# Thirty-two experts in pairs: a tensor engine program written out with constant waits, its block bounds read one pair ahead

## The reference, cut to what matters

```python
for e in range(N_EXPERTS):                      # 32
    hid = jax.nn.silu(t @ w_gate[e]) * (t @ w_up[e])     # 1024 -> 256
    out = out + combine[:, e:e + 1] * (hid @ w_down[e])  # 256 -> 1024
```

## Time and profile before

| | |
|---|---|
| runs | 565.57 us median of 3 (564.02 to 568.11) |
| the profiled execution's own time | 564.8 us |
| its span | 563.0 us (1.8 us lie around it) |
| PE busy | 489.6 us, 87% |
| DMA moved | 141.69 MB, 252 GB/s over the span |
| mean granted TensorE clock | 0.959 |

### The profile page before, as it was taken

One profiled execution on the slowest core, in us unless ns is written; L12 is line 12 of the kernel. 1 busy time (PEld: TensorE's weight loads), 2 busy tenths in 40 slices (PEclk: granted clock), 3 DMA queues, 4 the chain that ended last, 5 costly groups with the idle time before them and its releaser, 6 DMA issues.

```text
span 563.0 us, 9101 instructions
## 1 busy us (share of the span) xinstructions
PE 489.6 (87%) x3407; PEld 294.1 (52%) x3408; DVE 247.8 (44%) x478; ACT 108.5 (19%) x230; POOL 187.2 (33%) x282
## 2 busy tenths in 40 slices
PE   6999999999999999996489889898878687388972
PEld 4887777777776455453244444444434343244430
DVE  4139999999945223368222212222121212022236
ACT  5130111111125211121122112121111112012214
POOL 2014728836768001110423333332313313033100
PEclk9999999999999999996799999999989989699988
DMA  8993016000003991029678999999999999998076
GB/s 331 333 399 57 0 57 243 2 0 1 1 1 118 376 415 42 37 87 401 220 293 286 366 383 403 397 398 391 396 384 382 391 394 390 396 402 353 30 284 227
DMA packets 35504, 141.69 MB, mean 252 GB/s; under 512 B 10194, under 2 KB 10210, under 8 KB 23193
## 3 DMA queue, kind: packets, MB, share of 16 engines
q1 hardware_dynamic: 29194, 127.91, 59.8%
q0 software_dynamic: 4960, 9.45, 5.2%
q10 hardware_dynamic: 1327, 4.01, 1.8%
HBM read 134.99 MB, written 13.17 MB: 263 GB/s over the span
## 4 chain that ended last, share of the span: by engine, by line
PE 69%; DMA 15%; DVE 4%; SPq 4%; issue 4%; ACT 3%; ACTq 0%; POOL 0%; POOLq 0%; DVEq 0%
PE bank L1218 25%; PE bank L1301 9%; PE bank L1412 9%; PE bank L1432 8%; PE bank L1407 7%; DMA region_x<-in_w_up 6%; DMA region_w<-in_w_up 5%; SPq L383 4%; PE bank L1211 3%; DMA out<-sb_rows 2%; PE bank L1398 2%; PE bank L1362 1%; PE bank L1422 1%; PE bank L1327 1%; DVE ua L1109 1%
## 5 line engine op out<-in xcount | busy, mean ns | idle before, releaser
L1218 PE MATMUL bank<-region_h,region_w 128*128 128x256 f32 (+1 forms) x576 | 140.6, 406 | 0.0
L1218 PEld LDWEIGHTS bank<-region_h,region_w 128*128 128x128 f32 x576 | 109.2, 190 | 29.8
L1109 DVE TENSOR_TENSOR ua<-ua,bank 128x128 f32<-128x128 f32 x30 | 8.6, 286 | 191.0 <-ACT ua L616 191.0
L1412 PE MATMUL bank<-region_w,z 128*32 128x256 f32 x512 | 47.1, 419 | 14.6 <-DMA region_w<-in_w_up 12.3
L1301 PE MATMUL bank<-region_w,z 128*128 128x512 f32 x128 | 56.7, 596 | 0.2 <-ACT z L559 0.2
L1432 PE MATMUL bank<-region_w,ua 128*32 128x512 f32 x344 | 51.9, 598 | 0.0
L772 POOL COPY gcol<-gidx 64x1 uint32 (+1 forms) x30 | 5.3, 178 | 135.3 <-DVE sb_rows L1104 135.3
L894 DVE SCALAR_TENSOR_TENSOR z<-ub,par,z 128x512 f32<-128x512 f32 x60 | 47.5, 791 | 0.0
L894 DVE SCALAR_TENSOR_TENSOR region_x<-ub,par,region_x 128x512 f32<-128x512 f32 x56 | 46.5, 831 | 0.0
L703 POOL TENSOR_TENSOR ub<-region_x 128x512 f32<-128x512 f32 x4 | 25.3, 6320 | 57.8 <-ACT ub L513 31.1
L1301 PEld LDWEIGHTS bank<-region_w,z 128*128 128x128 f32 x128 | 23.8, 190 | 28.0 <-issue 26.3
(11 more groups left out here) (231 smaller groups left out, 628.3 us busy)
## 6 DMA issues: line engine op xcount, KB each, us to landing
region_w<-in_w_down SPq DMA_DIRECT2D x21, 1024.0 KB, 18.2
region_w<-in_w_gate SPq DMA_DIRECT2D x16, 1024.0 KB, 15.1
region_w<-in_w_up SPq DMA_DIRECT2D x16, 1024.0 KB, 17.1
region_w<-in_w_in SPq DMA_DIRECT2D x4, 2048.0 KB, 18.6
slot<-in_w_gate SPq DMA_DIRECT2D x6, 1024.0 KB, 14.8
slot<-in_w_up SPq DMA_DIRECT2D x6, 1024.0 KB, 14.4
slot<-in_w_down SPq DMA_DIRECT2D x6, 1024.0 KB, 14.8
region_x<-in_w_up SPq DMA_DIRECT2D x5, 1024.0 KB, 26.7
```

What stands on the lines that cost most here:

```text
L1218: ins = mm(ps[2 * bank + j][:, 0:LEN[j]], sec[name][:, k, c * P:(c + 1) * P], hT[:, k, CUT[j]], start=(k == 0), stop=(k == KC - 1))
L1412: ins = mm(ps[1][r0:r0 + H, 0:2 * P].rearrange("p (w f) -> p w f", w=2), xT[:, k, half * H:(half + 1) * H], wgu[i][:, :, k, h, :], start=( ...
```

## The change

- On TensorE the loop over slots goes. All 16 pairs are written out, and every wait on a weight has a constant (`turn_of(e) * 16 + 16`). The inner loops over own blocks stay, and so do their `If`s.
- The three reads of `bound` at the start of each pair go. The first pair's two bounds are read ahead of the wait for the first tokens (`mine = bounds(0)`); its first block is the constant 0, and later each pair's first block is the pair before's end, which is in a register. The bounds of pair m+1 are read in the shared block of pair m, behind the token transposes and ahead of the wait for the hidden rows.
- On SP the 26 reloads are written out, with constant slots, constant expert numbers in the DMAs' addresses and a constant place in `bound`. Each still reads one bound, waits as before and issues the same three DMAs in the same order.

```diff
             def load_part(i, part, e):
                 dst = ...
-                sp.dma_start(dst, parts[part][:, bass.ds(e, 1), :].rearrange("p e n -> p (e n)"))\
-                  .then_inc(s_wexp[i][part], 16)
+                sp.dma_start(dst, parts[part][:, e, :]).then_inc(s_wexp[i][part], 16)
...
-            with sp.Fori(1, NE // NSLOT) as it:
-                for i in range(NSLOT):
-                    reload(it, i)
-            for i in range(NE % NSLOT):
-                reload(NE // NSLOT, i)
+            for e in range(NSLOT, NE):
+                last = sp.value_load(bound[0:1, e - NSLOT + 1:e - NSLOT + 2], min_val=1, max_val=NBLK)
+                sp.wait_ge(s_gu, last)
+                load_part(slot_of(e), 0, e)
+                load_part(slot_of(e), 1, e)
+                sp.wait_ge(s_down, last)
+                load_part(slot_of(e), 2, e)
...
+            def bounds(m):
+                return [pe.value_load(bound[0:1, 2 * m + j:2 * m + j + 1], min_val=1, max_val=NBLK) for j in (1, 2)]
...
                 tr(ps[2][:, 0:P], hid, ident[:, :]).then_inc(s_hT_ps, 1)
                 tokens(KC // 2, KC).then_inc(s_xt_ps, 1)
+                ahead = meanwhile() if meanwhile else None
                 pe.wait_ge(s_hidT, g + 1)
...
             keep_busy(18)
             pe.wait_ge(s_tab, 1)
+            mine = bounds(0)
             pe.wait_ge(s_mv, 1)
             tokens(0, KC).then_inc(s_xt_ps, 1)
...
-            def pair(it, i):
-                e = it * NSLOT + i
-                first = pe.value_load(bound[0:1, bass.ds(e, 1)], min_val=0, max_val=NBLK - 1)
-                after = pe.value_load(bound[0:1, bass.ds(e + 1, 1)], min_val=1, max_val=NBLK)
-                end = pe.value_load(bound[0:1, bass.ds(e + 2, 1)], min_val=1, max_val=NBLK)
+            def pair(m, first, after, end):
+                e = 2 * m
...
-                block_of(after - 1, (i, i + 1), it)
+                ahead = block_of(after - 1, (e, e + 1), (lambda: bounds(m + 1)) if m + 1 < NPAIR else None)
...
-            with pe.Fori(0, NE // NSLOT) as it:
-                for i in range(0, NSLOT, 2):
-                    pair(it, i)
-            for i in range(0, NE % NSLOT, 2):
-                pair(NE // NSLOT, i)
+            first = 0
+            for m in range(NPAIR):
+                after, end = mine
+                mine = pair(m, first, after, end)
+                first = end
```

More of the change, by code:

```diff
@@ L87, in build_step, with slot_of, turn_of @@
                   (RX, D, ub_t, D)]
+        def slot_of(e):
+            return e % NSLOT
+        def turn_of(e):
+            return e // NSLOT
         slot_gu = [reg[:, lo:lo + 2 * PART] for reg, lo, _, _ in places]
@@ L1399, in tokens, with block_of @@
                 return ins
-            def block_of(g, halves, turn):
+            def bounds(m):
+                return [pe.value_load(bound[0:1, 2 * m + j:2 * m + j + 1], min_val=1, max_val=NBLK) for j in (1, 2)]
+            def block_of(g, experts, meanwhile=None):
+                halves = [slot_of(e) for e in experts]
                 pe.wait_ge(s_xt, g + 1)
@@ L1423, in block_of @@
                 tokens(KC // 2, KC).then_inc(s_xt_ps, 1)
+                ahead = meanwhile() if meanwhile else None
                 pe.wait_ge(s_hidT, g + 1)
                 pe.wait_ge(s_yc, g + 1)
-                for i in sorted(set(halves)):
-                    pe.wait_ge(s_wexp[i][2], turn * 16 + 16)
+                for e in sorted(set(experts)):
+                    pe.wait_ge(s_wexp[slot_of(e)][2], turn_of(e) * 16 + 16)
                 for c in range(F // P):
@@ L1435, in block_of @@
                 ins.then_inc(s_down, 1)
+                return ahead
             keep_busy(18)
             pe.wait_ge(s_tab, 1)
+            mine = bounds(0)
             pe.wait_ge(s_mv, 1)
             tokens(0, KC).then_inc(s_xt_ps, 1)
-            def pair(it, i):
-                e = it * NSLOT + i
-                first = pe.value_load(bound[0:1, bass.ds(e, 1)], min_val=0, max_val=NBLK - 1)
-                after = pe.value_load(bound[0:1, bass.ds(e + 1, 1)], min_val=1, max_val=NBLK)
-                end = pe.value_load(bound[0:1, bass.ds(e + 2, 1)], min_val=1, max_val=NBLK)
+            def pair(m, first, after, end):
+                e = 2 * m
                 for part in range(2):
-                    pe.wait_ge(s_wexp[i][part], it * 16 + 16)
+                    pe.wait_ge(s_wexp[slot_of(e)][part], turn_of(e) * 16 + 16)
                 with pe.If(after > first + 1):
                     with pe.Fori(first, after - 1) as g:
-                        block_of(g, (i, i), it)
+                        block_of(g, (e, e))
                 for part in range(2):
-                    pe.wait_ge(s_wexp[i + 1][part], it * 16 + 16)
-                block_of(after - 1, (i, i + 1), it)
+                    pe.wait_ge(s_wexp[slot_of(e + 1)][part], turn_of(e + 1) * 16 + 16)
+                ahead = block_of(after - 1, (e, e + 1), (lambda: bounds(m + 1)) if m + 1 < NPAIR else None)
                 with pe.If(end > after):
                     with pe.Fori(after, end) as g:
-                        block_of(g, (i + 1, i + 1), it)
-            with pe.Fori(0, NE // NSLOT) as it:
-                for i in range(0, NSLOT, 2):
-                    pair(it, i)
-            for i in range(0, NE % NSLOT, 2):
-                pair(NE // NSLOT, i)
+                        block_of(g, (e + 1, e + 1))
+                return ahead
+            first = 0
[3 more added lines that the diff above has]
+                first = end
             pe.wait_ge(s_diag, 2 * len(BY_PE))
```

## The result

The changed kernel takes 570.6 us (median of 14 runs, 568.13 to 574.64), the one before 567.92 us (14 runs on the same chips): ratio 1.0047, 95% interval 1.0024 to 1.0070. Measured again on another chip it was 573.48 against 566.51 us: 1.0128 (1.0106 to 1.0151). So it is slower, by 0.5% to 1.3%; the forecast was 0.2% faster. The measured 570.6 us lies inside the forecast range of 560.5 to 573.5, but on the other side of the kernel before.

A forecast was written before the change was run, and what follows sets the result against it. The weight stream through full DMA engines was taken as the bound. -2.4 us up to expert 8's issue and +1.4 us for code packets gave -1.0 us: 564.6 us from 565.57, range 560.5 to 573.5.

The forecast's parts named there:

- The first block starts earlier: Ahead of the first shared block, bounds read before the first tokens' wait remove most of 2.27 us of issue: gain 2.2 us.
- Reads in the shared block: Two reads ahead of the down matmuls show about 1.0 us in each shared block but the last.
- the first pair's end: The 1.18 us of issue at the end of the first pair goes whole, counted as -1.2 us.
- Up to the second release: From the start to expert 8's issue, at the second pair's shared block: -2.4 us, issue at 303.3 instead of 305.74.
- SP's part nothing: SP's written-out reloads gain nothing: same 26 reads, waits and DMAs in the same order, 0.33 to 0.35 us an issue.
- Longer code: PE's written-out pairs bring 20 more instruction packets of 1.14 us each into the full weight stream: +1.4 us.
- I take the spread: In the weight stream, the extra packets are taken as spread over 16 DMA engines, 1.4 us, not 22.8 on one.
- The argument from 372 against 394 GB/s: Windows with packets, 306 to 345, moved 5.6% less; half of six packets on one engine would have cost 9%.
- Rival 1: PE waits 1.5 us for code at each of 20 jumps over skipped own blocks: +7.8 us, 573.4; chance 0.13.
- a milder form of it: Smaller code stalls at jumps over own blocks, staying within 1%: a third of Rival 1's chance of 0.13.
- 0.6 us of margin: In the last pair, PE reaches its wait about 0.6 us before the weights land.

The follow-up runs named there:

- with fillers: Changed kernel with next pair's bounds read behind the down matmuls, plus 12 filler matmuls ahead of the last pair's weight wait: 1.0045 of the kernel before.
- the longer loop: Kernel before with a never-entered branch over 150 matmuls (300 instructions) at each pair's start: 692.21 us against 566.89, ratio 1.2200.

## Why the prediction was wrong

The sum was -1.0 us, and the time went up by 2.7 and by 7.0 us. The bound that it named, the weight stream, was right, and so, in the main, were these steps.

- *The first block starts earlier*: forecast 2.2 us, measured 1.7 (278.40 to 280.25 against 273.74 to 277.33). The rest is nearly all in the first tokens' transposes, which now take 1.08 us instead of 0.69.
- *Reads in the shared block*: forecast 1.0 us, measured mostly 0.8 to 0.95; the first pair's end 1.2 us less, as forecast.
- *Up to the second release*: forecast -2.4, measured -1.6 to -2.8.
- *SP's part nothing*: so in the stage; 1.9 us of time outside it stays unexplained.

**The step that failed is "Longer code".** The number of packets was right (20 more forecast, 21 found), and so was their length (1.14 us forecast, 1.05 found), but "I take the spread" over 16 engines was not: by the shares they go to eight. That makes 21 x 1.05 / 8 = 2.8 us instead of 1.4, and the sum +0.4 us instead of -1.0: the wrong sign comes from here, but not the whole size. The stream grew by 4.0 to 5.2. The rest is in the whole stream, not in the eight alone: the first of the 16 shares of the last up part came 212.7 and 211.4 us after expert 8, against 210.1 and 210.3 in the unchanged kernel, and the 8 KB packets took 338 and 337 ns on average against 334. Why, is open. This part is not in every profile: with fillers, 24 packets, the first share came at 210.4 us, the 8 KB packets took 335 ns, and the stream grew by 3.1 to 3.3 us, close to what eight engines give. The argument from 372 against 394 GB/s excluded one engine, and I read it as if it had excluded everything but 16. Over all profiles with a loop that stays or with no loop, the stream is 212.6 to 213.7 us with 3 or 4 packets, 213.9 with 10, 214.6 with 15 and 216.7 to 218.6 with 23 or 24. It grows with the packets, though from 15 on faster than in proportion.

**Rival 1 was half true.** The forecast had a chance for a milder form of it, and no price. It priced all 20 jumps alike and set against them that the first turn's took 0.35 us. In the written-out kernel most still take no more than 0.43, but two of the 16 branches of L1452 took 5.15 and 3.89 us in one execution (5.24 and 0.99 in the other). They are the same two in all five profiles of TensorE's fully written-out code, in the ninth pair (3.6 to 5.3 us) and in the last (0.6 to 3.9): late code comes in a few long stops, and not in many short ones. Why these two, and why a stop lasts longer than a packet's 1.05 us, is open. In the last pair nothing hides such a stop. I had given PE 0.6 us of margin there, without a row; even the unchanged kernel came 1.3 us late once.

The Trainium skill ("Runtime: NRT & Kernel Launch", Instruction fetch mechanics) says that a taken branch to a target outside the window at hand waits until the target is fetched. The 5.7 us a jump of the longer loop agree with it. The same section names this as a reason why kernels prefer full unrolling. Here the runs show the reverse: the loop of three pairs needed no instruction packet from 345 to 519, the written-out code needed 21 more than it in the stream, and the time rose by 0.5% to 1.3%.

**A third cost was not thought of at all.** PE stands for its code or its weights ahead of the last shared block (2.4 us in the changed kernel), and finds it at the low clock: 5.47 us for a block of 3.92, which puts 1.6 us on the path. Over the stream its granted clock falls a little too (0.93 against 0.95 and 0.94); there it is hidden.

Sum for the two profiles of the changed kernel against the first of before: -1.9 and -2.8, +5.2 and +4.3, 0 and +2.5, +1.9 and +1.1: +5.2 and +5.1 us, or 0.9%, between the two measured ratios. Against the second profile of before, which was itself 2.2 us longer behind the tokens, it is +3.0 and +2.9 us, 0.5%.

## What to carry to other kernels

Writing a loop out trades a register read at each turn for a stream of code. Look whether the loop was resident before (no instruction packets after its first turn), and, when the weights' DMAs are the bound, count the new packets against the engines that carry them: by these runs eight, not 16. Take only the turns whose time counts: here four of sixteen pairs, with their bounds read where the engine waits anyway, gave 0.5%, and all sixteen cost up to 1.3%. Give PE spare time ahead of its last block, where nothing hides a late jump. A loop of some 1300 instructions stayed resident and one of some 2200 did not (estimates, as above), so a rarely taken path inside a loop can cost more than it looks.

## What was not expected of the hardware

- PE's instruction packets (16 KB, about 1.05 us) went to eight of the 16 DMA engines: the shares of the later eight fell 3.0 us further behind those of the earlier eight with 20 or 21 more packets.
- A jump over 300 instructions in a loop that was not resident cost 5.7 us in the median and 6.7 at most (the loop's back edge up to 7.4), while a packet itself takes about 1 us. Jumps over 116 instructions mostly cost 0.2 to 0.4 us, and at two places 0.6 to 5.3.
- After a stop of 2.4 us the last shared block ran in 5.47 us (527.21; granted 0.88 in 527.2 to 541), and in 3.83 us at 1.00 where twelve filler matmuls stood in the stop.
